# Moving the low halves of the weights 24 bytes on in a float32 two-block kernel

## The reference

```
mod = silu(c) @ w_ada + b_ada                  # scales and shifts of the norms
h = modulate(rms_norm(x), sh1, sc1)
p = h @ w_in                                    # 1024 -> 9232: q, k, v, z, gates, short convolution
o = gated delta rule over q, k, v               # 8 heads, chunks of 64, a triangular solve
mix = (gate_a * (o @ w_gdn_proj) + gate_b * (conv(...) @ w_sc_out)) @ w_o
x = x + g1 * mix
x = x + g2 * ((silu(h2 @ w_g) * (h2 @ w_u)) @ w_ffn_out)   # h2 = modulated norm of x; width 2816
x = modulate(rms_norm(x), shf, scf)
# second block
q, k, v = rms_norm(x) @ w_qkv                   # 16 heads, attention with a relative bias
x = x + attention(q, k, v) @ w_o2
x = x + (silu(conv(u_gate)) * conv(u_val)) @ w_down        # u = rms_norm(x) @ w_up
return rms_norm(x)
```

## Time and profile before

| | |
|---|---|
| median of three runs | 913.4 us |
| profiled execution | 921.88 us |
| its span, first to last instruction | 920.1 us |
| granted TensorE clock, mean | 0.993 of full |
| PE busy | 893.8 us, 97% |
| DVE busy | 667.6 us, 73% |
| ACT busy | 505.1 us, 55% |
| HBM read | 174.29 MB |

### The profile page before, as it was taken

The page is one execution under the profiler, slowest core; times in us unless marked ns, Lnnn a source line. Parts: engine busy times, 40 slices in busy tenths (PEclk is TensorE's granted clock), DMA queues, the critical chain, the costliest instruction groups (busy, mean ns, idle before and its releaser), DMA issues.

```text
span 920.1 us, 18632 instructions
## 1 busy us (share of the span) xinstructions
PE 893.8 (97%) x8020; PEld 850.1 (92%) x8020; DVE 667.6 (73%) x1132; ACT 505.1 (55%) x814; POOL 65.8 (7%) x83
## 2 busy tenths in 40 slices
PE   5998999999999999999999999999999999999997
PEld 2798998999898999999999999999899999999997
DVE  4878767566978677677798775588665688778652
ACT  2489667454354627555354444466665576666442
POOL 0100201021001001020000000120000200000011
PEclk9999999999999999999999999999999999999999
DMA  8754233333767665465988889526331455555631
GB/s 335 279 191 162 102 129 104 128 138 109 259 232 247 209 229 179 165 217 179 288 326 295 287 287 255 218 96 226 138 138 53 177 184 192 190 192 178 223 126 46
DMA packets 27681, 177.31 MB, mean 193 GB/s; under 512 B 2864, under 2 KB 5680, under 8 KB 7504
## 3 DMA queue, kind: packets, MB, share of 16 engines
q1 hardware_dynamic: 27600, 176.13, 54.7%
HBM read 174.29 MB, written 1.84 MB: 191 GB/s over the span
## 4 chain that ended last, share of the span: by engine, by line
PE 82%; DVE 8%; ACT 6%; DMA 2%; issue 1%; DVEq 0%; SPq 0%; ACTq 0%
PE ps L1093 46%; PE ps L1099 22%; PE ps L1091 2%; DVE wl L1841 2%; DVE acc L1740 1%; ACT wh L1454 1%; PE ps L1138 1%; PE ps L1146 1%; PE ps L1232 1%; PE ps L1149 1%; PE ps L1097 1%; DMA raw<-in_ada_dram 1%; PE ps L1252 1%; PE ps L1303 1%; DMA raw<-in_w_sc_dram 1%
## 5 line engine op out<-in xcount | busy, mean ns | idle before, releaser
L1093 PE MATMUL ps<-HH,wh 128*128 128x256 f32 x1480 | 374.1, 288 | 0.7 <-DVE wl L1841 0.2
L1841 DVE TENSOR_TENSOR wl<-raw,wh 128x1024 fp32r<-128x1024 f32 x265 | 320.2, 1228 | 73.4 <-ACT wh L1454 72.8
L1093 PE MATMUL ps<-HH,wl 128*128 128x256 f32 x1480 | 361.0, 279 | 0.0
L1454 ACT ACTIVATE wh<-raw 128x1024 fp32r<-128x1024 f32 x265 | 273.8, 1043 | 142.5 <-PE ps L1099 112.9
L1093 PEld LDWEIGHTS ps<-HH,wh 128*128 128x128 f32 x1480 | 280.4, 189 | 9.8 <-issue 4.3
L1093 PEld LDWEIGHTS ps<-HH,wl 128*128 128x128 f32 x1480 | 279.8, 189 | 1.9 <-issue 1.9
L1099 PE MATMUL ps<-HL,wh 128*128 128x256 f32 x1480 | 229.1, 279 | 0.3 <-DVE HL L1786 0.3
L1099 PEld LDWEIGHTS ps<-HL,wh 128*128 128x128 f32 x1480 | 197.1, 189 | 0.6 <-DVE HL L1786 0.5
L1093 PE MATMUL ps<-FH,wh 128*128 128x256 f32 x352 | 85.9, 278 | 0.0
L1093 PE MATMUL ps<-FH,wl 128*128 128x256 f32 x352 | 85.9, 278 | 0.0
L1740 DVE SCALAR_TENSOR_TENSOR acc<-raw,silc,acc 128x512 f32<-128x512 f32 x101 | 76.3, 756 | 8.0 <-DMA raw<-in_ada_dram 4.9
(11 more groups left out here) (269 smaller groups left out, 1080.9 us busy)
## 6 DMA issues: line engine op xcount, KB each, us to landing
raw<-in_ada_dram SPq DMA_DIRECT2D x32, 1024.0 KB, 5.2
raw<-in_w_fi_dram SPq DMA_DIRECT2D x22, 1024.0 KB, 4.9
raw<-in_w_up_dram SPq DMA_DIRECT2D x22, 1024.0 KB, 4.8
raw<-in_w_rest_dram SPq DMA_DIRECT2D x20, 1024.0 KB, 4.8
raw<-in_w_in_dram SPq DMA_DIRECT2D x16, 1024.0 KB, 4.8
raw<-in_w_qkv_dram SPq DMA_DIRECT2D x12, 1024.0 KB, 4.8
raw<-in_w_o_dram SPq DMA_DIRECT2D x8, 1024.0 KB, 4.8
raw<-in_w_fo_dram SPq DMA_DIRECT2D x8, 1024.0 KB, 5.0
```

Source lines behind the costliest of these rows:

```text
L1093: e.matmul(o, w[:, k, 128 * t:128 * t + 128], x_hi[:, k0 + k, :], start=first and n + k == 0, **MM)
L1454: e.activation(whl[u % HALF][0][:, 0:n], raw[i % RAW][:, c:c + n], ACT.Copy).then_inc(*a_hi.up(u))
L1841: e.tensor_tensor(wl[:, 0:n], raw[i % RAW][:, c:c + n], wh[:, 0:n].bitcast(F32), ALU.subtract).then_inc(*v_lo.up(u))
```

## The change

The five `wh` and five `wl` are no longer ten tensors but parts of one tensor `W`: the five high ones first, each 1024 elements long, then a space of 6 elements (24 bytes), then the five low ones. `W` has 8 elements more than the ten had, which moves X on by 32 bytes, and `home_x` is 32 bytes shorter, so that HH and all that is declared after it stays where it was. Addresses divided by 512 leave now: wh 128, wl 152, X 160, and the rest as before. With the rows at 64, wh lies 64 past them and wl 88. The number and order of the instructions are the same on every engine; line numbers behind the change grow by 2.

```diff
--- before.py
+++ after.py
@@ -206,10 +206,12 @@
 
     psum = [ctx.enter_context(nc.psum_tensor(f"ps{i}", [128, 512], F32)) for i in range(BANKS)]
     raw = [sb(f"raw{i}", [128, 2048]) for i in range(RAW)]
-    whl = [(sb(f"wh{i}", [128, 1024], F32R), sb(f"wl{i}", [128, 1024], F32R)) for i in range(HALF)]
+
+    W = sb("W", [128, 2048 * HALF + 8], F32R)
+    whl = [(W[:, 1024 * i:1024 * i + 1024], W[:, 1024 * (HALF + i) + 6:1024 * (HALF + i) + 1030]) for i in range(HALF)]
     X = sb("X", [128, 8, T])
 
-    sb("home_x", [128, 112])
+    sb("home_x", [128, 104])
     HH = sb("HH", [128, 8, T], F32R)
     HL = sb("HL", [128, 8, T], F32R)
     vec = sb("vec", [128, NVEC])
```

## The result

The changed kernel is slower: median 925.2 us against 915.0 (twelve runs of each), ratio 1.0098, 95% interval 1.0077 to 1.012. Run again later beside other kernels (e16) it was at 1.0071, 1.0042 to 1.01. So it lost 0.7 to 1.0%, where 0.8% had been forecast as a gain. Its profiled execution took 926.41 us with a span of 924.6.

A forecast was written before the change was run, and what follows sets the result against it. TensorE's product matmul spacing was taken as the bound; winning 12 of the slow pace's 15.2 us gave 909.9 us profiled, scaled to 901.5, or 908.4 if the last block was already fast; 906 was taken between, range 898 to 922.

The forecast's parts named there:

- The reading of what bounds the kernel: TensorE, busy in 97% of the span: time follows the distance between product matmul starts, 113.3 ns fast or 117.8 slow.
- The terms put at nothing: X moved by 32 bytes, 0 us within 0.2; DVE's shifted wl write, 0, at worst 1.3 us hidden; load near 189 ns.
- The size of what there was to win: Product matmuls: 0.55 of 6264 in the slow pace at 4.4 ns, 15.2 us, of which 7.0 in the last block.
- The step that failed: Product matmuls: a wl load 24 bytes off interrupts the slow pattern and the fast pace stays, winning 12 of 15.2 us.
- rival (a): Product matmuls: pace is drawn at each interruption and held whatever the distance; 913.4 us within 3; chance 0.25.
- Rival (b): Product matmuls: fast pace needs every load alike, wl loads break it; 12.4 us to 925, or 917.5; chance 0.28.
- Its second way: TensorE's wl loads: 33 pieces of 16 bytes, not 32, 5.9 ns on 2024 loads, 11.9 us to 925; within (b)'s 0.28.
- Rival (c): TensorE's wl loads also lose part of a fixed excess, 5.0 ns on 2024 matmuls, 10 us more, 896; chance 0.05.
- the step from 921.88 to the median: Whole kernel: 909.9 scaled by 913.4 / 921.88 to 901.5; if unprofiled last blocks were already fast, only 5 us won, 908.4.

The follow-up runs named there:

- e16: The changed kernel unaltered, timed again beside other kernels against the kernel before: median 921.8 us, ratio 1.0071.
- e1: Against the changed kernel, the 24 bytes of space lie behind the low weights, so all weights stay at 64, X still moved: 916.5 us, ratio 1.0011 to the kernel before.
- e6: The changed kernel (64 / 88) with TensorE taking four wh and then four wl for the high rows: 912.6 us, ratio 0.9974 to the kernel before.
- e7: The kernel before (all weights at 64) with four wh and then four wl for the high rows: 917.4 us, ratio 1.0046 to the kernel before.
- e8: Against the changed kernel, low weights at 320 past the rows, high ones at 64, alternating: 915.2 us, ratio 1.0011 to the kernel before.
- e5: The changed kernel with the two places exchanged, high weights at 88 and low at 64, alternating: 920.1 us, ratio 1.0052 to the kernel before.
- e2: Against the changed kernel, high and low weights both at 88 past the rows, alternating order: 913.1 us, ratio 0.9975 to the kernel before.
- e15: Against the changed kernel, weight buffers 0, 2, 4 at 64 and 1, 3 at 88, so distance changes only from unit to unit: 912.8 us, ratio 0.9973 to the kernel before.
- e13: Against the changed kernel, high and low weights both at 80 past the rows, alternating order: 934.9 us, ratio 1.0214 to the kernel before.
- e12: Against the changed kernel, high and low weights both at 96 past the rows, alternating order: 931.5 us, ratio 1.0167 to the kernel before.
- e14: All weights at 88 past the rows, with four wh and then four wl for the high rows: 914.9 us, ratio 1.0004 to the kernel before.

## Why the prediction was wrong

The reading of what bounds the kernel held: nothing but the distance between product matmuls moved, the waits and the other engines stayed, and excess and span went together in seventeen variants. The terms put at nothing held: X (e1), DVE's shifted write (1229 against 1228 ns), and the load itself (189 ns).

The size of what there was to win held too: 15.2 us had been put on the slow pace, and the excess of the profiled execution is 14.3, of which 7.0 lie in the last block, as forecast.

The step that failed is this one: that a wl load standing 24 bytes off would interrupt the slow pattern, after which the fast pace stays. The change was to win 12 of those 15.2 us; the excess grew by 4.8. I took the stretches of product matmuls that nothing interrupts and went through each by the sum of three distances (under 343 ns fast, over 350 slow). Nearly all begin slow, in the kernel before (106 of 118) as in the changed one (113 of 119). In the kernel before 57 then fall to the fast pace, in the changed one 36, nearly always within the first ten matmuls, and none goes back. At their end (the last six distances under 114.4 ns on average) 67 of 115 are fast before, 42 of 115 in the changed kernel and 39 of 119 in e16. So the alternating loads did not end slow stretches, they kept them: fewer fall, and those that don't are in new patterns. The steady one, 117.2 ns, repeats every twelve matmuls. It is a little quicker than the old slow one (the last block won 0.8 us), and in the profiled execution it holds where the fast one was before (345 to 415 us, the down-projection).

What the step describes does exist, in another order: in e6, where the distance changes twice in twelve matmuls, 12 of the 15 long stretches that are slow from the 10th to the 16th matmul have fallen to the fast pace by the 39th, most of them near the 32nd. In the changed kernel, where it changes eight times, none of 14 does, and in e7, where it never changes, 2 of 9. The forecast was right that a change of distance can end a slow stretch, and wrong that one at nearly every matmul would.

Which pace a stretch gets is not fixed by the kernel. The three longest stretches hold 2608 of the 6264 product matmuls; their mean distances in ns, one execution each:

| kernel | from 355 us, 492 matmuls | from 540 us, 539 | last block, 1577 |
|---|---|---|---|
| before | 113.3 | 113.4 | 117.8 |
| e1 | 113.4 | 113.3 | 117.8 |
| e7 (64, grouped) | 117.8 | 117.8 | 113.3 |
| e8 (64 / 320) | 117.8 | 113.3 | 113.3 |
| changed | 117.2 | 117.3 | 117.2 |
| e16 (changed again) | 113.4 | 117.3 | 117.2 |
| e5 (88 / 64) | 116.7 | 116.7 | 116.7 |
| e2, e15 | 113.4 | 113.4 | 113.4, 113.3 |
| e13 (80 / 80) | 118.7 | 118.7 | 118.7 |

With all weights at 64 each of the three was seen in either pace (e7 in the grouped order), so rival (a) had part of it right: a pace is taken after an interruption and then mostly held. What (a) had wrong is that the distance doesn't matter.

Held only mostly: one stretch exchanges its operands on the way (from 627 us in the kernel before, 47 matmuls and then twelve of the v2 product). Before, e1, e7 and e8 cross that place in the fast pace (113.3 ns ahead of it, 113.5 behind). In e5, e6 and e16 the pace is 113.3 ns up to within three matmuls of it, and 119.5, 116.4 and 116.5 ns behind it, with no interruption. So a change of how loads and rows stand to each other can also end the fast pace, which is the opposite of what the forecast had it do.

Rival (b) gave this sign, place and size: 12.4 us to 925, with 925.2 measured and a loss of 9 to 10 us by the ratio. That the number meets is in part luck: every product was to go at the slow pace of 117.8 ns, and the mean in the trace is 116.5. Its reason, that the fast pace needs every load to stand alike, is not what the runs show. In e6 and e15 loads at 64 and 88 mix and the fast pace is there, in the last block from end to end; in the changed kernel itself there are stretches with both at 113.3 ns. What costs is their alternation from one matmul to the next (changed, e16, e5), with either of the two at 88: it makes the fast pace rarer. And it is these two distances that do it, since 64 and 320 alternate in e8 for nothing.

Its second way, one more piece of 16 bytes for each load, was wrong. The Trainium skill (SBUF — State Buffer, Specifications (TRN2)) gives lines of 16 bytes with a penalty at each cross to a new one; at 88, where a row of weights touches one line more, e2 has no loss, and at 80 and 96, where it doesn't, e13 and e12 lose 2.1 and 1.7%. So lines crossed do not sort these kernels. The prediction read the page too narrowly as well: the same row asks for two hits or more in a line for full bandwidth, and a start 8 bytes into a line still leaves two elements of 4 bytes in the first and in the last line, so it does not plainly forecast a loss at 88.

Rival (c) had no ground. Rows 12 compare a transpose with a plain matmul, and I let the difference in their loads speak for distance. No stage of any placement tried had a mean below 113.3 ns.

The forecast also leaned on the step from 921.88 to the median. I had weighed that other runs might have the last block in the fast pace. The last block's 7.0 us off 921.88 leave 914.9, and the median is 915.0. The trace of e1, with weights placed as before, has that block slow at 920.66 us; the profiled executions of e2, e6, e8 and e15 have it fast and took 912.4 to 913.3, that of e14 too, with 914.2, and of e7 with 917.9, where the other two long stretches are slow. This fits medians of the kernel before at 914 to 918 with single runs up to 924, but an execution of the kernel before with a fast last block was not profiled. It would explain why the two profiled executions lie 4.5 us apart and the medians 10.2.

What stays open: why 64, 88 and 320 allow the fast pace and 80 and 96 do not. The alignment to 16, 32 or 64 bytes does not sort them, and 112 and 128 were only tried for the low weights. Why alternating costs between 64 and 88 and not between 64 and 320 is open too. What in the array or its reads repeats every twelve matmuls was not found, and what decides the pace in the first starts of a stretch wasn't either.

## What to carry to other kernels

When one engine is full, look at the distance from start to start of its instructions in several stretches, and not at the mean of the kernel: two paces in the same line say that something other than work and waits sets it. Where weights lie relative to the streamed rows is such a thing; 16 bytes on for all weights made the kernel 2% slower, and a place that is good for all loads can be bad when it alternates with another good one. Test a placement for all loads, for some, and in another order, before giving a reason for it; a profile of one execution may be in another pace than the median, so judge by many executions and use the profile to see what differs.

## What was not expected of the hardware

- Product matmuls of 128x256 lie 113.3 ns apart or 117.8, at the same clock, addresses and shapes, and the slow pace holds for up to 185 us on end (725.6 to 911.2 us in the kernel before). Within an uninterrupted stretch the pace falls from slow to fast, in the kernel before and the changed one nearly always in the first ten matmuls. It was seen to rise only with 64 and 88 mixed, in the stretches with the v2 product (e5, e6, e16; a longer last distance at the end of a stretch is left out).
- With all weights at 88 that exchange is dear too: in e2 the twelve matmuls behind it lie 119.4 ns apart, against 113.5 with all at 64.
- With all weights at 80 or 96 past the rows (modulo 512 bytes) the mean is 118.7 or 118.2 ns and the fast pace is absent; count in 50 us of the last block for both at 96, where the fast pace has 444:

```profile
800.00:850.00 50.00, 50.00 (x424) 1.00 0.54 187
```

- Grouped by four, 64 and 88 together bring slow stretches back to the fast pace: in e6 12 of 15 that were slow from the 10th to the 16th matmul are fast by the 39th, with all at 64 in the same order 2 of 9.
- With distances 64 and 88 the changed kernel keeps 429, with the same two by unit 444:

```profile
800.00:850.00 50.00, 50.00 (x444) 1.00 0.56 197
```

- e6 and e15 beat both kernels, by 0.26 and 0.27% of the kernel before; the upper ends of their intervals are 0.9993 and 0.9998, so the gain is about as small as can be told.
